# A hybrid attention/SSD layer on one core: all rows of x loaded at once, two sets of temporaries, another product order, other first loads of the second block

## What is computed

```
h = rms_norm(x, norm_gain)
q, k, v, z_a, z_s, xbc, dt, gates = split(h @ w_in)       # 1024 -> 8480 columns
o_a = window_attention(rope(rms_norm(q)), rope(rms_norm(k)), v, sinks)   # 128 frames, chunks of 64
branch_a = (o_a * silu(z_a)) @ w_attn_proj
y_s = ssd_mixer(silu(causal_conv4(xbc)), softplus(dt))    # chunked scan, 32 heads, state 64 x 128
branch_b = rms_norm(y_s * silu(z_s)) @ w_ssd_proj
out = x + (sigmoid(g_a) * branch_a + sigmoid(g_b) * branch_b) @ w_out
```

## Time and profile before

| | us |
|---|---|
| median of 3 runs (lowest, highest) | 1418.75 (1415.56, 1422.06) |
| profiled execution | 1417.91 |
| its span | 1416.1 |
| first product of Block 1 starts | 68.9 |
| Block 2 starts on PE | 502.2 |
| PE busy from 580 to 660 (a pass of Block 2), clock | 80.00 of 80, 1.00 |
| last projection of Block 2 ends, Block 3 starts | 1036 |

### The profile page before, as it was taken

The page is one execution under the profiler, slowest core; times in us unless marked ns, Lnnn a source line. Parts: engine busy times, 40 slices in busy tenths (PEclk is TensorE's granted clock), DMA queues, the critical chain, the costliest instruction groups (busy, mean ns, idle before and its releaser), DMA issues.

```text
span 1416.1 us, 20612 instructions
## 1 busy us (share of the span) xinstructions
PE 1358.4 (96%) x7108; PEld 1088.0 (77%) x7108; DVE 782.6 (55%) x955; ACT 612.1 (43%) x1148; POOL 585.1 (41%) x344
## 2 busy tenths in 40 slices
PE   5698999999999979999999999999999999998999
PEld 4686777888888857888787878888768888776787
DVE  4775777676666455536554555555365554555311
ACT  5545444545444343435252535344356533323110
POOL 3443564445544423333333233333336666443321
PEclk9899999999999989999999999999999999999999
DMA  5331644422323276778666785869586265334431
GB/s 201 144 90 66 191 138 134 178 103 99 110 104 119 103 183 157 189 199 157 202 154 203 164 210 151 238 150 202 129 296 235 104 218 196 136 139 158 146 106 59
DMA packets 166500, 221.59 MB, mean 156 GB/s; under 512 B 7760, under 2 KB 127824, under 8 KB 166208
## 3 DMA queue, kind: packets, MB, share of 16 engines
q1 hardware_dynamic: 130640, 172.64, 43.0%
q10 hardware_dynamic: 35728, 48.37, 9.4%
q0 software_dynamic: 96, 0.13, 0.0%
HBM read 152.57 MB, written 63.31 MB: 152 GB/s over the span
## 4 chain that ended last, share of the span: by engine, by line
PE 84%; issue 5%; POOL 3%; DVE 3%; DMA 2%; ACT 2%; SPq 0%; ACTq 0%; POOLq 0%; DVEq 0%
PE F L180 37%; PE F L930 28%; PE F L1772 3%; PE M L1772 3%; PE M L1093 2%; PE M L1136 2%; DMA sb_early<-x_d 2%; POOL sb_res L1596 1%; PE F L1130 1%; PE F L1123 1%; PE F L1107 1%; PE M L1130 1%; PE M L1123 1%; PE F L1725 1%; PE F L899 1%
## 5 line engine op out<-in xcount | busy, mean ns | idle before, releaser
L180 PE MATMUL F<-sb_xb,sb_whl 128*128 128x512 f32 x1536 | 376.3, 402 | 0.0
L180 PEld LDWEIGHTS F<-sb_xb,sb_whl 128*128 128x128 f32 x1536 | 286.9, 188 | 75.2 <-issue 9.2
L192 POOL TENSOR_TENSOR sb_whl<-sb_wst,sb_whl 128x1024 fp32r<-128x1024 f32 x64 | 159.3, 2490 | 405.6 <-ACT sb_whl L189 405.3
L180 PE MATMUL F<-sb_X,sb_whl 128*128 128x512 f32 x1104 | 259.7, 396 | 5.9 <-issue 3.0
L180 PEld LDWEIGHTS F<-sb_X,sb_whl 128*128 128x128 f32 x1104 | 206.5, 187 | 58.5 <-issue 8.2
L930 PE MATMUL F<-sb_tv,sb_whl 128*128 128x512 f32 x1008 | 242.4, 396 | 2.3 <-DVE sb_acc L734 2.3
L930 PEld LDWEIGHTS F<-sb_tv,sb_whl 128*128 128x128 f32 x1008 | 189.2, 188 | 49.3 <-issue 3.1
L414 POOL TENSOR_TENSOR sb_whl<-sb_acc,sb_whl 128x512 fp32r<-128x512 f32 x103 | 145.7, 1421 | 135.8 <-ACT sb_whl L461 135.8
L930 PE MATMUL F<-sb_xb,sb_whl 128*128 128x512 f32 x756 | 187.6, 401 | 7.5 <-POOL sb_whl L414 5.7
L930 PEld LDWEIGHTS F<-sb_xb,sb_whl 128*128 128x128 f32 x756 | 142.7, 190 | 46.3 <-POOL sb_whl L414 7.6
L189 ACT ACTIVATE sb_whl<-sb_wst 128x1024 fp32r<-128x1024 f32 x64 | 67.6, 1058 | 198.4 <-DMA sb_wst<-w_units 97.1
(11 more groups left out here) (216 smaller groups left out, 1776.5 us busy)
## 6 DMA issues: line engine op xcount, KB each, us to landing
...
```

The costliest lines, as they stand in the source:

```text
L180: last = nc.tensor.matmul(bank, weight(slot, wp, k), act(ap, k, half), start=(k == 0 and wp == 0 and ap == 0), stop=(k == NK - 1 and wp == 1))
L192: return nc.gpsimd.tensor_tensor(weights(slot, 1), raw_unit(slot), weights(slot, 0).bitcast(f32), ALU.subtract)
```

## The change

Six things move at once.

1. Rows of x are loaded to eight places of their own in `early` (the memory that later holds `TV`), in pieces of 512 B; only SP's queue orders them. `v_in1` loads go ahead of the second tile.
2. There are two sets of `ttmp`; `b12_copy(q)` waits for `t_lo` of quarter q-2.
3. The low part of the dt weights moves from POOL to DVE; ACT makes the first v high part ahead of tile 1's square; each projection comes one tile later on PE.
4. In a pair products 4 and 5 change places: the one that needs `u3_done` comes first. ACT now makes both splits of the next pair ahead of `c11`, which waits for product 5 instead of product 4. `take_c21` waits for product 4 instead of 5.
5. Block 2: the loads start after product 4 of the last pair instead of product 1; `bc` is loaded ahead of `csb` in all eight passes.
6. The state is cleared on POOL; PE waits for it only before `off(0)`.

```diff
-            tv, blk = ((None, 0), (2, None), (3, None), (0, None), (None, 2), (1, None), (None, 3))[idx]
+            tv, blk = ((None, 0), (2, None), (3, None), (0, None), (1, None), (None, 2), (None, 3))[idx]
...
             load_x(0)
-            load_x(1)
...
-            load_x(2)
-            for n in range(3, NT):
-                sp.wait_ge(xt_done, n - 2)
+            load_x(1)
+            for n in range(2, NT):
                 load_x(n)
-                if n == 4:
-                    sp.wait_ge(v_lo, 3)
-                    load_raw(0)
+            sp.wait_ge(v_lo, 2)
+            load_raw(0)
...
             def b12_copy(q):
-                if q:
-                    act.wait_ge(t_lo, q)
-                else:
+                if q >= 2:
+                    act.wait_ge(t_lo, q - 1)
+                elif q == 0:
                     act.wait_ge(pads_in, 48)
...
             def c11(n):
-                act.wait_ge(prod, 7 * n + 5)
+                act.wait_ge(prod, 7 * n + 6)
...
+                if n + 1 < NPAIR:
+                    split(n + 1, 0)
+                    split(n + 1, 1)
                 c11(n)
...
-                if n + 1 < NPAIR:
-                    split(n + 1, 0)
-                    split(n + 1, 1)
...
             def take_c21(n):
-                dve.wait_ge(prod, 7 * n + 6)
+                dve.wait_ge(prod, 7 * n + 5)
...
             for n in range(NT):
                 transpose_x(n)
-                if n == 1:
-                    pe.wait_ge(v_lo, 3)
-                if n >= 1:
-                    project_vdt(n - 1)
+                if n == 2:
+                    pe.wait_ge(v_lo, 2)
+                    pe.wait_ge(dt_lo, 1)
+                if n >= 2:
+                    project_vdt(n - 2)
+            project_vdt(NT - 2)
             project_vdt(NT - 1)
...
                 if idx >= 4:
-                    pe.wait_ge((u2_done, u3_done, c22_done)[idx - 4], at * c + (n + 1))
+                    pe.wait_ge((u3_done, u2_done, c22_done)[idx - 4], at * c + (n + 1))
...
-            sp.wait_ge(prod, 7 * (NPAIR - 1) + 2)
+            sp.wait_ge(prod, 7 * (NPAIR - 1) + 5)
...
-            dve.wait_ge(c12_done, NPAIR)
-            nc.vector.memset(state[:], 0.0).then_inc(state_ready, 1)
+            dve.sem_inc(state_ready, 1)
...
+            pool.wait_ge(c12_done, NPAIR)
+            nc.gpsimd.memset(state[:], 0.0).then_inc(state_zero, 1)
```

More of the change, by code:

```diff
@@ L218, in build @@
         block = root.enter_context(nc.Block())
-        xrow, w = carve(acc_all, 2 * NK * VD, 3, DM)
+        ttmp2, w = carve(acc_all, 2 * NK * VD, 4, 4, P)
+        sums, w = carve(acc_all, w, 2, HALF)
         cst1, w = carve(acc_all, w, NCONST - BLOCK1_CONSTS)
@@ L231, in build @@
         gqs, w = carve(acc_all, w, 2, T)
-        sums, _ = carve(acc_all, 2 * NK * VD + 2 * DM, 2, HALF)
-        ttmp, _ = carve(part_all, 0, 4, 4, P)
+        ttmp1, _ = carve(part_all, 0, 4, 4, P)
+        ttmp = (ttmp1, ttmp2)
         zpad, _ = carve(part_all, 0, 256)
@@ L292, in x_block, with xrow @@
             return halves[:, :, i // 4, part_, :, (i % 4) * P:(i % 4 + 1) * P]
+        def xrow(n):
+            rows = early.rearrange("p a (s k t) -> p (a s) k t", s=2, k=NK)
+            return rows[:, n % 4, :, (2 + n // 4) * P:(3 + n // 4) * P]
         def t_block(part_, q, lo=0, hi=4):
@@ L311, in operand @@
         def operand(n, idx):
-            return (raw_w(n, 0, 0), sums[:, 1, :], raw_w(n, 1, 0), sums[:, 0, :], raw_w(n, 0, 1), raw_w(n, 1, 1), sums[:, 1, :])[idx]
+            return (raw_w(n, 0, 0), sums[:, 1, :], raw_w(n, 1, 0), sums[:, 0, :], raw_w(n, 1, 1), raw_w(n, 0, 1), sums[:, 1, :])[idx]
         def conv_acc(u):
@@ L461, in split, with square_x, v_high @@
                 nc.scalar.activation(ring(idx, 0), operand(n, idx), ACT.Copy).then_inc(p_hi, 1)
[L463 to L465 removed]
+            def square_x(n):
+                if n < 2:
+                    act.wait_ge(x_in[n], 16)
+                else:
+                    act.wait_ge(x_in[n // 2 + 1], 32)
+                nc.scalar.activation(whl[:, 3 * DM:4 * DM].rearrange("p (k c) -> p k c", c=P), xrow(n), ACT.Square,
+                                     accum_out=ssx[:, 0, n:n + 1]).then_inc(x_sq, 1)
                 act.wait_ge(x_sq, n + 1)
                 nc.scalar.activation(ssx[:, 0, n:n + 1], ssx[:, 0, n:n + 1], ACT.Sqrt, bias=eps[:], scale=1.0 / DM).then_inc(x_rt, 1)
+            def v_high(u):
+                act.wait_ge(v_in1, 32)
+                nc.scalar.activation(vw[:, 0, :, u * P:(u + 1) * P], raw_unit(u).rearrange("p (k c) -> p k c", k=NK),
+                                     ACT.Copy).then_inc(v_hi, 1)
+            for n in range(NT):
                 if n == 1:
[L469 to L472 removed]
+                    v_high(0)
+                square_x(n)
+                if n == 1:
+                    v_high(1)
                     nc.scalar.activation(vw[:, 0, :, 2 * P:VD], dtraw[:], ACT.Copy).then_inc(v_hi, 1)
@@ L1054, in _ @@
                 sp.wait_ge(dec_ready, j * 4 + 1)
+                sp.wait_ge(yg_done, j * 4 + 1)
+                sp.dma_start(bc[:], x_d[16:24, :, ds(at_j, P)].rearrange("n p t -> p n t")).then_inc(bc_in, 16)
                 for p in range(2):
```

47 lines of the change are left out of this document (22 added, 25 removed).

## The result

| | before | changed |
|---|---|---|
| median of the runs taken together | 1418.83 us | 1449.07 us |
| profiled execution, its span | 1417.91, 1416.1 | 1451.1, 1449.3 |

A forecast was written before the change was run, and what follows sets the result against it. PE works 425.9 of 430 us in the product stage, so only the first product's start, new waits in the pairs and Block 2's start count. -6.0 + 17.3 - 5.2 = +6.1 gave 1424.5 us, range 1410 to 1434.

The forecast's parts named there:

- Rows of x: Stage up to the first product: sums of x start earlier, first product at 62.9 instead of 68.94, -6.0 us.
- the ring: Quarters of x sums, DVE and POOL: stays, period 11.4, since DVE's row multiplication (3.36) waits for POOL's low part.
- the last quarter's 9.3: Rows of x: the last quarter comes 9.3 us behind the third, taken as set by PE's projections.
- Pairs 1 and 2: Product stage: the product needing L734's sum now stands first; waits +5.6, slower clock after the idle +4.0.
- Pairs 4 to 7: q pairs: c11 ahead of post_b shifts L734 by 1.2; PE waits 1.4 or 2.5 in each, 7.7 us together.
- the clock unharmed: Pairs 4 to 7: such short waits cost no clock, since after 1.34 twelve matmuls took 3.04.
- Start of Block 2: Wait for the clearing (3.04) ends, but loads come about 1.4 later behind the later gate: +0.6 us.
- First pass: Block 2: bc wait of 6.92 goes; causal +1.5, clock -1.5, a weight unit's wait +1.1.
- Passes 2 to 8: Block 2: later csb and weight units are held by some 5.5 us of slack, so 0, but near the edge.
- C: Rival, passes 2 to 8: PE waits 2 us in each of 7 for csb or decayed x; 1438, chance 0.13.
- B: Rival, product order: the swap costs little, DVE reaches L734 before product 3 ends; -8, at 1410, chance 0.20.
- D: Rival, rows of x: the ring breaks, quarters take 9.9 instead of 11.8, 5.6 more gained; 1419, chance 0.17.

The follow-up runs named there:

- e5: The kernel of e3 with one set of temporaries for the sums of x again: ratio 0.9988.
- e13: Changed kernel storing one of 16 blocks of y per pass, with POOL's multiplication of x by d_skip behind the next low part: 1461.11 us, ratio 1.0315.
- e14: Changed kernel, full y store, with POOL's multiplication of x by d_skip moved behind the next low part: 1479.82 us, ratio 1.0447.
- e8: The kernel of e3 with the wait for yg_done put ahead of csb, bc behind csb: 1432.45 us, ratio 1.0074.
- e1: Changed kernel with the old order of the products alone taken back: 1420.81 us, ratio 1.0025.
- e2: Changed kernel with csb again ahead of the wait for yg_done and of bc in all passes: 1435.40 us, ratio 1.0130.
- e3: Changed kernel with both undone, old product order and csb ahead of the yg_done wait and bc: 1411.02 us, ratio 0.9959.
- e6: The kernel of e3 with bc ahead of csb in the first pass of Block 2 alone: ratio 0.9953.
- e7: The kernel of e6 with the loads of Block 2 after product 1 of the last pair again: ratio 0.9952.
- e11: Changed kernel with ACT's post_b of a q pair ahead of c11 instead of behind it: 1434.80 us in one run.
- e12: The kernel of e3 with the rows of x multiplied by the reciprocal root alone, norm_gain left out: 1414.95 us in one run.

## Why the prediction was wrong, step by step

- **Rows of x (-6.0):** right, -6.3, and right at each quarter to 0.3. Right also that the ring does not break, since L713 waits out POOL; the "about 1.3" without POOL stands in no line of the earlier trace rows, but the trace before has it (1.28). But the last quarter's 9.3 was ascribed to PE's projections alone, and e5 shows that it takes the second set (2 us).
- **Pairs 1 and 2 (+9.6):** right. The waits grew by 5.8 (forecast 5.6), and the slow restarts cost some 3.1 (taken 4.0, from bounds of 0 and 6).
- **Pairs 4 to 7 (+7.7):** the mechanism was right, the size too small. 10.1 of waits and about 2.9 of slower matmuls make 13.0. Two terms were mis-sized. "L734 1.2 later" left out that a shifted row of DVE meets other instructions of POOL: in pairs 4 and 6 the wait is 2.5, not 1.4. And "the clock unharmed", taken from a wait of 1.34, was put at nothing for waits of 2.5, two of which cost 1.4 and 1.5.
- **Start of Block 2 (+0.6):** the loads came later than taken. The gap is 4.94, 1.9 more than before. With the 0.9 that the first product gave back, these rows add up to the stage's +22.8 within 0.1.
- **First pass (-5.8):** -3.9. `causal` did take the place of the wait for `bc`, with 4.19 instead of 1.5, mostly because POOL's L1456 stretched it by 2.1. The clock gave back 1.1 (taken 1.5), and the wait of 1.1 for a weight unit isn't in the trace.
- **Passes 2 to 8 (0):** this step failed, by 20.8. The term was put at nothing on a slack of 5.5, found by following `csb` and the weight units along SP's queue to DVE and PE. What I never counted was the store of y, which is on ACT's queue. It landed 31.2 after its issue in the first case (593.94), 16.2 before (581.29). POOL's L1456 waits for it, starts 11 to 12 late, and stretches DVE's `causal` ahead of the `diag` products. That is 12.7 of the 20.8 (e13 and e14 take the collision away with `csb` nearly as late, and the first part is 36.4 again), and the lower clock behind these waits 4.9 more. The counted path failed as well, for some 3: L1278 starts 5.3 later in pass 3, which the slack of 5.5 would have held, but POOL's low part stretches it by 1.7.

The later `csb` alone doesn't explain the late store, as e8 shows (8.5 behind `csb`, landed after 18.5). What goes with it in every pass of the traces is the load of z on SP's queue. Before, z stood behind `bc`, whose issue took 9.49, and was issued just behind the store:

```profile
581.29 1.10 ACTq L1406 DMA_DIRECT2D y_d<-sb_acc  x1
582.53 2.13 SPq L1061 DMA_DIRECT2D sb_early<-z_d  x1
```

With `bc` ahead, z follows `csb` at once and is issued ahead of the store:

```profile
587.76 12.55 SPq L1081 DMA_DIRECT2D sb_early<-z_d  x1
...
593.94 2.09 ACTq L1426 DMA_DIRECT2D y_d<-sb_acc  x1
```

In the whole kernels that load `csb` in one piece (before, changed, e1 to e3, e5 to e8, e11, e12, e14), all 54 stores of 1 MB with z issued behind them landed after 14.7 to 19.5, between 0.2 ahead of z and 2.9 behind it. All 28 with z issued 6 or more ahead landed after 27.6 to 31.2, within 0.7 of the first half of `ecsb`, the next load behind. Two stores of the old order fell between, with z issued 0.0 and 0.4 ahead: 19.6 in e2, and 25.5 in e3, where POOL then waited 7.3. No run moved z alone, so that z's place is the cause isn't shown.

Of the rivals, C named the stage and even the edge ("the slack is of the size of the shift"), but with 14 us and by data that come late; of its two edges, `csb` and the decayed x, the second came true for some 3 us. Its chance of 0.13 was too low, and the range ended where it began. B and D did not come true: the new order saved DVE nothing, and the ring held. The chance of 0.36 for slower should have been the larger one, since two of the five steps stood on slacks of a few us and both could only err upwards.
